# Feed-forward input unscaled, its first 256 columns multiplied tile by tile, the row scale applied behind the product

## Chip, cores and metric

One core of a Trainium2 chip runs the kernel alone. The metric is device time in microseconds (us), the median of the runs shown. Engines: PE (TensorE; PEld its weight loads), DVE (VectorE), ACT (ScalarE), POOL (GpSimd), SP (SyncE, which issues most DMAs).

## What is computed

One decoder layer on 512 prompt rows and 32 sample rows: T = 544 tokens, width 2048, all in 32 bits. A mixer sublayer, then

```
def rmsnorm(x, g):
    y = xf * lax.rsqrt(jnp.mean(xf * xf, axis=-1, keepdims=True) + EPS)
    return y * g
x = x + rmsnorm(out, g_post)                 # end of the mixer
h = rmsnorm(x, g_pre)                        # feed-forward
a = square(relu(einsum('ntd,df->ntf', h, w_up)))      # 2048 -> 8192
y = x + rmsnorm(einsum('ntf,fd->ntd', a, w_down), g_post)
```

## The kernel before

Activations lie transposed: 16 tiles of 128 features by 544 tokens. Every 32-bit product is made of three passes over numbers split into a high and a low part (high x high, high x low, low x high); ACT writes high parts, DVE writes low parts as source minus high. The projections before the feed-forward (up to 578 us) are plain: one unit of weights is 4 tiles by 256 columns.

**Feed-forward.** `w_up` goes in 32 groups of 256 columns, and each group is a Strassen-Winograd product of 2x2 blocks: 7 products (i = 0 to 6, numbered N = 7 G + i), each 8 x 3 matmuls of 272 columns. The block sums of the weights are made by POOL (`t1`, `t3`, `t2`, `t4`, L737 to L756), those of the activations once (`h_sum`, L1504, 8 x 272 = 2176 elements a row), then every part is split (`h_high`, `h_low`, L1509; for weights `high_copy`, `high_part`, `low_part`, L1445). After each product DVE reads the bank (`take`, L1462 and L1465) and adds it to one of four quadrants (`quads`). Products 0, 2, 4 and 6 of a group accumulate in one bank, so product 2 may start only when product 0 has been taken (`taken_before`). At a group's end `square_relu` (L1472, L1474) squares the quadrants, POOL forms their block sums (`activation_sums`, L762 to L767), ACT the high part (`mlp_high`, L1037), DVE the low part (`mlp_low`, L1479), and SP stores both to DRAM (`store_hi`, `store_lo`). `w_down` follows in 64 groups of 7 half-size products.

DVE's order in the up stage is written out by hand; i = 6 is the last product of a group:

```
for N in range(3, N_UP):
    take(N)
    low_part(N + 3)
    if i == 3 and G > 0: mlp_low(G - 1)
    if i == 6: square_relu(G)
```

**Between mixer and feed-forward** (578 to 642 us) the squares of the out-projection are summed by POOL (`add`, L709) and by PE (`turn_sums`), `row_roots` makes the row scale, PE spreads it over the partitions (`spread_scales`), and then tile by tile: POOL or DVE scales the tile, PE transposes the residual input (`second_turn`, 5 transposes, L1595), DVE adds both (L1437), ACT squares, POOL adds the squares. A second row scale comes out of these, `scale_tiles` (L1493) applies it with the gain, and only then the block sums, the splits and the first product begin.

## Time and profile before

| | us |
|---|---|
| median of 3 runs (lowest, highest) | 2060.28 (2059.46, 2060.66) |
| the profiled execution's own time | 2059.49 |
| its span in the trace | 2057.7 |
| PE busy | 1974.6 (96%) |
| DVE, ACT, POOL busy | 1329.2, 1222.3, 926.7 |
| mean granted TensorE clock | 0.971 |

The span is cut by stage with busy times of all engines; a row of the timeline gives start, length, engine, line, and in brackets how long the engine had been idle and what released it. L numbers are lines of the kernel before. A granted clock (PEclk) of 1.00 is 2.4 GHz, 0.50 is 1.2 GHz.

### The profile page before, as it was taken

Reading aid. Unit: us, or ns where it says so; the run is one execution under the profiler, and the core shown is the slowest. Engines: PE = TensorE matmul, PEld = TensorE weight load, DVE = VectorE, ACT = ScalarE, POOL = GpSimd, SP = SyncE. Lnnn points to the kernel's source line nnn. Section 1 sums busy time; section 2 is a strip of 40 time slices with the busy share of each in tenths; the row PEclk is TensorE's granted clock in tenths of the full one; section 3 lists DMA queues with packets and bytes.
Section 4 is the critical chain, followed back from the end, with each engine's and each line's share of the span. In section 5 each row is a group of like instructions: output and inputs, shape, how many; then the busy total and the mean of one; then the engine's idle time right before and its main releaser. Section 6 shows DMA issues by size and latency. Waiting matters only on the chain.

```text
span 2057.7 us, 39370 instructions
## 1 busy us (share of the span) xinstructions
PE 1974.6 (96%) x15412; PEld 1946.8 (95%) x15412; DVE 1329.2 (65%) x1975; ACT 1222.3 (59%) x1787; POOL 926.7 (45%) x635
## 2 busy tenths in 40 slices
PE   7999999999974999999999999989999999999998
PEld 7999999899954899999999999989999999999998
DVE  3455642622247777777777777766666666666687
ACT  5244421422224577777777777767777777777784
POOL 0000022211152576767677676744445544444472
PEclk9999998999965999999999999999999999999999
DMA  5421121242310556565665656795656556565542
GB/s 178 157 68 57 52 78 57 79 173 86 103 65 22 161 187 209 178 200 184 190 199 184 212 178 199 225 328 190 209 181 203 183 180 206 190 212 187 182 159 88
DMA packets 270766, 328.15 MB, mean 159 GB/s; under 512 B 8128, under 2 KB 236872, under 8 KB 268975
## 3 DMA queue, kind: packets, MB, share of 16 engines
q1 hardware_dynamic: 267104, 315.66, 47.1%
q10 hardware_dynamic: 3479, 9.99, 1.4%
q8 instruction: 123, 2.02, 0.4%
q14 instruction: 60, 0.49, 0.1%
HBM read 253.79 MB, written 74.22 MB: 159 GB/s over the span
## 4 chain that ended last, share of the span: by engine, by line
PE 91%; DVE 4%; POOL 2%; issue 1%; DMA 1%; ACT 0%; SPq 0%; DVEq 0%; POOLq 0%; ACTq 0%
PE banks L1629 21%; PE banks L1984 21%; PE banks L1986 21%; PE banks L1985 21%; PE banks L1774 1%; POOL sq_sum L709 1%; PE banks L1595 1%; PE banks L1744 1%; PE banks L1762 1%; DVE h_part L1509 1%; DVE x1T L1493 1%; DVE h_sum L1504 0%; DMA mlp_kept<-mlp_sums 0%; PE banks L2002 0%; PE banks L1816 0%
## 5 line engine op out<-in xcount | busy, mean ns | idle before, releaser
L1984 PE MATMUL banks<-h_part,splits 128*128 128x272 f32 x1792 | 524.4, 293 | 26.9 <-DVE h_part L1509 16.1
L1984 PE MATMUL banks<-mlp_parts,splits 128*128 128x272 f32 x1792 | 518.3, 289 | 5.4 <-DVE y_sum L1462 3.7
L1986 PE MATMUL banks<-h_part,splits 128*128 128x272 f32 x1792 | 522.7, 292 | 0.0
L1985 PE MATMUL banks<-h_part,splits 128*128 128x272 f32 x1792 | 520.2, 290 | 0.0
L1986 PE MATMUL banks<-mlp_parts,splits 128*128 128x272 f32 x1792 | 517.7, 289 | 0.0
L1985 PE MATMUL banks<-mlp_parts,splits 128*128 128x272 f32 x1792 | 516.8, 288 | 0.0
L1984 PEld LDWEIGHTS banks<-h_part,splits 128*128 128x128 f32 x1792 | 341.7, 191 | 28.0 <-issue 19.7
L1984 PEld LDWEIGHTS banks<-mlp_parts,splits 128*128 128x128 f32 x1792 | 337.3, 188 | 6.2 <-issue 3.9
L1985 PEld LDWEIGHTS banks<-h_part,splits 128*128 128x128 f32 x1792 | 342.3, 191 | 0.0
L1985 PEld LDWEIGHTS banks<-mlp_parts,splits 128*128 128x128 f32 x1792 | 341.5, 191 | 0.0
L1986 PEld LDWEIGHTS banks<-h_part,splits 128*128 128x128 f32 x1792 | 341.4, 191 | 0.0
L1986 PEld LDWEIGHTS banks<-mlp_parts,splits 128*128 128x128 f32 x1792 | 337.3, 188 | 0.0
L1465 DVE TENSOR_TENSOR y_sum<-y_sum,banks 128x272 f32<-128x272 f32 x416 | 182.1, 438 | 184.5 <-PE banks L1986 184.4
L1629 PE MATMUL banks<-acts_hi,w_hi 128*128 128x272 f32 x1184 | 253.3, 295 | 9.4 <-DVE uT L1185 4.1
L1629 PE MATMUL banks<-acts_lo,w_hi 128*128 128x272 f32 x1184 | 247.0, 290 | 0.0
L1629 PE MATMUL banks<-acts_hi,w_lo 128*128 128x272 f32 x1184 | 247.0, 290 | 0.0
L803 ACT ACTIVATE w_hi<-w_raw 128x1024 fp32r<-128x1024 f32 x74 | 78.3, 1059 | 283.3 <-PE banks L1629 276.3
L1103 DVE TENSOR_TENSOR w_lo<-w_raw,w_hi 128x1024 fp32r<-128x1024 f32 x74 | 101.5, 1373 | 199.2 <-ACT w_hi L803 198.9
L1629 PEld LDWEIGHTS banks<-acts_hi,w_hi 128*128 128x128 f32 x1184 | 188.0, 191 | 15.5 <-issue 12.3
L1028 ACT ACTIVATE splits<-t_y 128x512 fp32r<-128x512 f32 (+1 forms) x192 | 148.5, 774 | 78.1 <-PE banks L1986 78.1
L1629 PEld LDWEIGHTS banks<-acts_lo,w_hi 128*128 128x128 f32 x1184 | 189.0, 191 | 0.0
L1629 PEld LDWEIGHTS banks<-acts_hi,w_lo 128*128 128x128 f32 x1184 | 187.3, 191 | 0.0
(234 smaller groups left out, 3453.7 us busy)
## 6 DMA issues: line engine op xcount, KB each, us to landing
raw_up<-in_w_up SPq DMA_DIRECT2D x128, 512.0 KB, 7.7
raw_down<-in_w_down SPq DMA_DIRECT2D x128, 512.0 KB, 4.4
mlp_parts<-mlp_kept SPq DMA_DIRECT2D x56, 1088.0 KB, 8.3
mlp_kept<-mlp_hi SPq DMA_DIRECT2D x32, 952.0 KB, 4.5
mlp_kept<-mlp_sums SPq DMA_DIRECT2D x32, 952.0 KB, 5.7
w_raw<-in_w_in SPq DMA_DIRECT2D x40, 512.0 KB, 3.5
w_raw<-in_w_out SPq DMA_DIRECT2D x32, 512.0 KB, 3.3
x_kept<-x1T SPq DMA_DIRECT2D x4, 1088.0 KB, 4.0
```

The lines of the kernel that those rows point to most:

```text
L709: nc.gpsimd.tensor_tensor(total[:], total[:], tmp[:, par * T:(par + 1) * T], ALU.add).then_inc(sq_added, 1)
L803: nc.scalar.activation(w_hi[:, k % SPLIT_SLOTS, :], w_raw[:, k % RAW_SLOTS, :], ACT.Copy).then_inc(hi_split, 1)
L1028: nc.scalar.activation(split_of(N, 0), weight_of(N), ACT.Copy).then_inc(part_hi, 1)
L1103: nc.vector.tensor_tensor(w_lo[:, k % SPLIT_SLOTS, :], w_raw[:, k % RAW_SLOTS, :], w_hi[:, k % SPLIT_SLOTS, :].bitcast(F32), ALU.subtract) ...
L1465: nc.vector.tensor_tensor(dst, dst, src, ALU.add).then_inc(taken, 1)
L1493: ins = nc.vector.scalar_tensor_tensor(out=x1T[:, kt, :], in0=x1T[:, kt, :], scalar=g_ffn[:, kt:kt + 1], in1=norm_scale[:], op0=ALU.mult, ...
L1509: nc.vector.tensor_tensor(h_parts[i][1][:], src, h_parts[i][0][:].bitcast(F32), ALU.subtract).then_inc(hp_lo, 1)
L1595: ins = nc.tensor.transpose(flat(2 * s, T)[:, c * P:c * P + r], tok[0:r, c, kt * P:(kt + 1) * P], ident[0:r, 0:r])
L1629: ins = nc.tensor.matmul(out[:, h, :], w, x[:, h * H:(h + 1) * H], start=first, stop=last)
L1984: nc.tensor.matmul(out, wh, xh, start=first, stop=False, skip_group_check=not STARTS[i])
L1985: nc.tensor.matmul(out, wh, xl, start=False, stop=False, skip_group_check=not STARTS[i])
L1986: ins = nc.tensor.matmul(out, wl, xh, start=False, stop=j == pairs - 1, skip_group_check=not STARTS[i])
```

## The change

The sublayer's input x1 is kept without its row scales: the out-projection gets only its gain; the residual input is multiplied by the row's root mean square instead (`rms`, by ACT, DVE and POOL, `scale_x`), so that x1T holds x1 divided by a row scale s1. Its epsilon is scaled (`eps_1`), s1 comes back at the very end (`s1_col`). Tiles are split high and low as they come (`tile_high`, `tile_low`), and the first 256 columns of `w_up` are multiplied plainly with them, 12 matmuls a tile (`plain_tile`), in place of the first Strassen group; 31 groups are left, on `w_up` columns from 256. The gain is applied to x1T in place (`gain`, POOL and ACT), the four block sums are made behind the plain part by DVE and POOL. The second row scale is summed at N = 4, spread at N = 6, and applied to the products (`ffn_scale`): `square_relu` is now relu times scale over four quadrants, then two squarings. For N < 14 the low part subtracts the high part in SBUF (`split_of`) rather than a copy in PSUM. Weight sum `t3` overwrites a block of the raw weights.

```
-    UP_GROUPS = F // UNIT_N
+    F_GROUPS = F // UNIT_N
+    UP_GROUPS = F_GROUPS - 1
...
+            sp.wait_ge(h_summed[0], 2)
+            sp.wait_ge(h_summed[1], 2)
...
+            blocks_split(0)
+            load_up(2)
+            store_hi(0)
+            store_lo(0)
+            for g in range(1, UP_GROUPS - 1):
+                store_hi(g)
+                store_lo(g)
...
+            def gain(kt):
+                gp.wait_ge(hp_hi, kt + 1)
+                gp.wait_ge(hp_lo, kt + 1)
+                gp.wait_ge(sq_ready, KT + kt + 1)
+                gp.wait_ge(x1_moved[kt // 2], 16)
+                nc.gpsimd.tensor_scalar(x1T[:, kt, :], x1T[:, kt, :], g_ffn[:, kt:kt + 1], None, ALU.mult).then_inc(gained[0], 1)
...
+                gp.wait_ge(t_ready, 4 * G + 1)
+                b12 = block_of(G, 0, 1)
+                nc.gpsimd.tensor_tensor(b12, block_of(G, 1, 1), b12, ALU.subtract).then_inc(t_ready, 1)
...
             t2(0)
+            a11, a12 = x1_quads[:, :, 0, 0, :], x1_quads[:, :, 1, 0, :]
+            a21 = x1_quads[:, :, 0, 1, :]
+            gp.wait_ge(gained[0], KT // 2)
+            gp.wait_ge(gained[1], KT // 2)
+            nc.gpsimd.tensor_tensor(s_sums[4][:], a11, a21, ALU.subtract).then_inc(h_summed[1], 1)
+            gp.wait_ge(unit_used, U_END)
+            gp.wait_ge(h_summed[0], 2)
+            nc.gpsimd.tensor_tensor(s_sums[5][:], a12, s_sums[2][:], ALU.subtract).then_inc(h_summed[1], 1)
             for G in range(ALL_G):
                 t4(G)
                 if 0 < G <= UP_GROUPS:
-                    activation_sums(G - 1)
+                    activation_sums(G)
                 if G + 1 < ALL_G:
                     t1(G + 1)
                     t3(G + 1)
+                    if G == 0:
+                        activation_sums(0)
...
+            def tile_high(kt):
                 act.wait_ge(x1_ready, kt + 1)
...
+                nc.scalar.activation(tile_parts(kt, 0), tile_halves(kt), ACT.Copy, scale=g_ffn[:, kt:kt + 1]).then_inc(hp_hi, 1)
...
+            for N, sums in ((1, (2, 0, 2)), (2, (3, 0, 1)), (3, (4, 1, 2)), (4, (5, 1, 2))):
                 high_copy(N)
                 high_part(N)
...
+                sum_high(*sums)
+            for N in range(5, N_ALL):
                 high_copy(N)
                 high_part(N)
                 G, i = divmod(N, NP)
...
+            step(nc.vector.tensor_copy(s1_col[:], rstd[:]))
+            step(nc.vector.tensor_scalar(eps_1[:], var[:], EPS, None, ALU.mult))
+            nc.vector.tensor_tensor(rms[:], var[:], rstd[:], ALU.mult).then_inc(rms_ready, 1)
...
+            def add_x(kt):
+                dve.wait_ge(x_turned, KT + kt + 1)
+                nc.vector.tensor_tensor(x1T[:, kt, :], x1T[:, kt, :], flat(2 * (kt % 2), T), ALU.add).then_inc(x1_ready, 1)
+            def tile_low(kt):
+                dve.wait_ge(x1_ready, kt + 1)
+                dve.wait_ge(hp_hi, kt + 1)
+                nc.vector.scalar_tensor_tensor(out=tile_parts(kt, 1), in0=tile_halves(kt), scalar=g_ffn[:, kt:kt + 1],
+                                               in1=tile_parts(kt, 0).bitcast(F32), op0=ALU.mult, op1=ALU.subtract).then_inc(hp_lo, 1)
+            def low_part(N):
+                if N >= HIGH_FROM:
+                    dve.wait_ge(hi_copied, N - HIGH_FROM + 1)
                 else:
...
+            def square_quads(g, a21):
+                dve.wait_ge(relued, g + 4)
+                nc.vector.tensor_tensor(mlp_sums[:, 0:3, :], quads[:, 1:4, :] if g > 0 else mlp_sums[:, 0:3, :],
+                                        quads[:, 1:4, :] if g > 0 else mlp_sums[:, 0:3, :], ALU.mult).then_inc(squared, 1)
+                nc.vector.tensor_tensor(a21, a21, a21, ALU.mult).then_inc(squared, 1)
             def square_relu(g):
-                dve.wait_ge(taken, NP * (g + 1))
-                if g > 0:
-                    dve.wait_ge(lo_stored, 16 * g)
-                nc.vector.scalar_tensor_tensor(out=mlp_sums[:, 0:3, :], in0=quads[:, 1:4, :], scalar=0.0, in1=quads[:, 1:4, :],
-                                               op0=ALU.max, op1=ALU.mult).then_inc(squared, 1)
-                nc.vector.scalar_tensor_tensor(out=quads[:, 0, :], in0=quads[:, 0, :], scalar=0.0, in1=quads[:, 0, :],
-                                               op0=ALU.max, op1=ALU.mult).then_inc(squared, 1)
+                dve.wait_ge(taken, NP * g)
+                by_half = quads[:].rearrange("p (a h) n -> p a h n", h=2)
+                nc.vector.scalar_tensor_tensor(out=by_half, in0=by_half, scalar=0.0,
+                                               in1=ffn_scale[:].unsqueeze(1).broadcast_to([P, 2, 2, H]),
+                                               op0=ALU.max, op1=ALU.mult).then_inc(relued, 1)
+                dve.wait_ge(lo_stored, 16 * g)
+                square_quads(g, quads[:, 0, :])
+            def square_relu_plain():
+                dve.wait_ge(h_summed[1], 2)
+                for out, bank, h in ((mlp_sums[:, 0, :], 6, 0), (mlp_sums[:, 1, :], 7, 1), (mlp_sums[:, 2, :], 4, 0),
+                                     (plain21[:], 5, 1)):
+                    nc.vector.scalar_tensor_tensor(out=out, in0=banks[:, bank, 0:H], scalar=0.0, in1=ffn_scale[:, 1 - h, :],
+                                                   op0=ALU.max, op1=ALU.mult).then_inc(relued, 1)
+                square_quads(0, plain21[:])
...
+            def sum_low(i, rounded):
+                dve.wait_ge(hp_hi, rounded)
+                nc.vector.tensor_tensor(s_parts[i][1][:], s_sums[i][:], s_parts[i][0][:].bitcast(F32), ALU.subtract).then_inc(hp_lo, 1)
+            add_x(0)
+            add_x(1)
+            for kt in range(KT):
+                tile_low(kt)
+                if kt + 2 < KT:
+                    add_x(kt + 2)
+                if kt == 5:
+                    split(U_FFN + 2)
+                if kt == 9:
+                    split(U_FFN + 3)
             low_part(0)
+            dve.wait_ge(gained[0], KT // 2)
+            dve.wait_ge(gained[1], KT // 2)
+            nc.vector.tensor_tensor(s_sums[3][:], x1_quads[:, :, 0, 1, :], x1_quads[:, :, 1, 1, :], ALU.add).then_inc(h_summed[0], 1)
+            dve.wait_ge(h_summed[0], 1)
+            nc.vector.tensor_tensor(s_sums[2][:], s_sums[3][:], x1_quads[:, :, 0, 0, :], ALU.subtract).then_inc(h_summed[0], 1)
             low_part(1)
+            dve.wait_ge(h_summed[0], 2)
+            sum_low(2, KT + 1)
             low_part(2)
             take(0)
+            sum_low(3, KT + 2)
+            take(1)
             low_part(3)
+            sum_low(4, KT + 3)
+            take(2)
             low_part(4)
+            sum_low(5, KT + 4)
+            take(3)
             low_part(5)
+            take(4)
+            low_part(6)
+            sums_by_token(2, banks[:, 1, :])
+            row_roots(2, eps_1)
+            take(5)
+            low_part(7)
+            dve.wait_ge(spread, 2)
...
+            dve.wait_ge(scale_ready, 4)
+            square_relu_plain()
+            take(6)
+            low_part(8)
+            low_part(9)
+            mlp_low(0)
+            square_relu(1)
+            for N in range(NP, N_UP):
...
                 G, i = divmod(N, NP)
-                if i == 3 and G > 0:
-                    mlp_low(G - 1)
+                if i == 3:
+                    mlp_low(G)
                 if i == 6:
-                    square_relu(G)
...
+            def plain_tile(kt):
...
+                for nt in range(2):
+                    for w, x, first, last in ((w_hi, 0, kt == 0, False), (w_hi, 1, False, False), (w_lo, 0, False, kt == KT - 1)):
+                        for h in range(2):
+                            ins = nc.tensor.matmul(out[:, h, :], w[s][:, cols], base[:, t + 2 * h, x, j, :], start=first, stop=last)
...
+            for kt in range(KT):
+                if kt + 2 < KT:
+                    second_turn(kt + 2)
+                plain_tile(kt)
...
+                if N == 4:
+                    turn_sums(2, banks[:, 1, :])
+                if N == 6:
+                    pe.wait_ge(rstd_ready, 3)
+                    spread_chunks(lambda c: banks[:, 1, c * P:(c + 1) * P] if c < TOK - 1 else banks[:, 4, 512 - ND:512])
+                if N == NP:
+                    pe.wait_ge(scale_ready, 4)
```

Where order moves. **DVE at the end of an up group, before** (`splits` are the parts of the weights, `quads` the quadrants):

```order
L1462 COPY quads<-banks 128x272 [waits a_summed,product_done]
L1445 TENSOR_TENSOR splits<-t_y,banks 128x1024 [waits product_done,hi_copied]
L1472 SCALAR_TENSOR_TENSOR mlp_sums<-quads 128x816 [waits lo_stored,taken]
L1474 SCALAR_TENSOR_TENSOR quads<-quads 128x272
L1462 COPY quads<-banks 128x272 [waits squared,product_done]
L1445 TENSOR_TENSOR splits<-t_x,banks 128x1024 [waits product_done,hi_copied]
```

The same place now:

```order
L1601 COPY quads<-banks 128x272 [waits a_summed,product_done]
L1582 TENSOR_TENSOR splits<-t_y,banks 128x1024 [waits product_done,hi_copied]
L1616 SCALAR_TENSOR_TENSOR quads<-quads,ffn_scale 128x1088 [waits taken]
L1608 TENSOR_TENSOR mlp_sums<-quads 128x816 [waits relued,lo_stored]
L1610 TENSOR_TENSOR quads<-quads 128x272
L1601 COPY quads<-banks 128x272 [waits squared,product_done]
L1582 TENSOR_TENSOR splits<-t_x,banks 128x1024 [waits product_done,hi_copied]
```

Between the last take of a group and the first take of the next stand three instructions over 2176 columns where two over 1088 stood.

**DVE behind the plain part, now** (`s_sum` block sums, `s_part` their halves):

```order
L1652 TENSOR_TENSOR s_sum_114<-x1T 128x2176 [waits gained_act,gained_pool]
L1654 TENSOR_TENSOR s_sum_113<-s_sum_114,x1T 128x2176 [waits h_summed_dve]
L1582 TENSOR_TENSOR splits<-raw_up_121,splits 128x1024 [waits unit_used,part_hi]
L1637 TENSOR_TENSOR s_part_1_106<-s_sum_113,s_part_0_105 128x2176 [waits hp_hi,h_summed_dve]
L1582 TENSOR_TENSOR splits<-t_y,splits 128x1024 [waits product_done,part_hi]
L1601 COPY quads<-banks 128x272 [waits product_done]
```

and **POOL at the same time**:

```order
L785 TENSOR_SCALAR x1T<-x1T,vecs 128x544 [waits sq_ready,x1_moved7,hp_lo,hp_hi]
L812 TENSOR_TENSOR t_x<-raw_up_121 128x1024 [waits raw_landed0]
L817 TENSOR_TENSOR raw_up_121<-raw_up_121 128x8x128 [waits t_ready]
L824 TENSOR_TENSOR t_y<-raw_up_121,t_x 128x1024 [waits t_ready]
L850 TENSOR_TENSOR s_sum_115<-x1T 128x2176 [waits gained_act,gained_pool]
L853 TENSOR_TENSOR s_sum_116<-x1T,s_sum_113 128x2176 [waits h_summed_dve,unit_used]
L830 TENSOR_TENSOR t_y<-raw_up_121,t_y 128x1024 [waits t_ready,part_lo,part_hi]
```

The low part of the second product's weights now stands behind two block sums on DVE, and two more block sums stand in POOL's queue ahead of `t4`.

## Rows read from the trace of the kernel before

**Rows 1.** The page: the chain that ended last, by engine.
```profile
PE 91%; DVE 4%; POOL 2%; issue 1%; DMA 1%; ACT 0%; SPq 0%; DVEq 0%; POOLq 0%; ACTq 0%
```

**Rows 2.** By stretch: busy PE, PEld, DVE, ACT, POOL; PEclk; DMA share; GB/s.
```profile
585.00:621.00 36.00, 19.23 (x73) 12.98 (x72) 21.98 (x25) 10.38 (x16) 32.19 (x23) 0.50 0.28 114
...
642.00:685.00 43.00, 29.86 (x168) 29.28 (x169) 38.08 (x30) 23.34 (x19) 9.85 (x5) 0.74 0.31 98
685.00:716.00 31.00, 28.74 (x216) 28.55 (x215) 21.98 (x23) 20.28 (x20) 20.46 (x11) 0.94 0.43 132
...
716.00:1330.00 614.00, 613.91 (x4868) 613.72 (x4867) 476.43 (x493) 448.48 (x435) 434.25 (x232) 1.00 0.62 192
```

**Rows 3.** Timeline (start, us, engine, line, tile): ACT, PE, DVE before the feed-forward.
```profile
577.96 0.62 ACT L977 ACTIVATE sq_tmp<-banks 128x544 f32<-128x544 f32 x1 [2.38 <-PE banks L1629]
...
577.76 2.29 PE L1595 MATMUL banks<-ident,x_tok 128*128 128x128 f32 x15
...
582.18 0.16 DVE L1119 COPY ss<-banks 128x4 f32<-128x4 f32 x1 [2.84 <-PE banks L1619]
...
583.89 0.17 DVE L1115 TENSOR_TENSOR rstd<-root,newton 128x5 f32<-128x5 f32 x1
...
587.57 1.35 PE L1595 MATMUL banks<-ident,x_tok 128*128 128x128 f32 x5 [0.82 <-DVE norm_scale L1126]
```

**Rows 4.** PE in the input projection's first pair, tile by tile.
```profile
29.96 1.53 PE L1595 MATMUL banks<-ident,x_tok 128*128 128x128 f32 x10
...
34.54 1.53 PE L1595 MATMUL banks<-ident,x_tok 128*128 128x128 f32 x10
```

**Rows 5.** Groups by shape: busy us, mean ns of one | idle before.
```profile
L1504 DVE TENSOR_TENSOR h_sum<-x1T 128x2176 f32<-128x2176 f32 x2 | 4.8, 2418 | 0.0
...
L737 POOL TENSOR_TENSOR t_x<-raw_up 128x1024 f32<-128x1024 f32 x32 | 77.1, 2410 | 14.6 <-DMA raw_up<-in_w_up 14.6
...
L709 POOL TENSOR_TENSOR sq_sum<-sq_sum,sq_tmp 128x544 f32<-128x544 f32 x30 | 42.4, 1412 | 168.1 <-ACT sq_tmp L977 167.0
...
L693 POOL TENSOR_TENSOR acts_lo<-qT,acts_hi 128x2176 fp32r<-128x2176 f32 x2 | 10.7, 5378 | 29.1 <-ACT acts_hi L947 29.1
...
L699 POOL MEMSET sq_sum<- 128x544 f32 x2 | 1.1, 560 | 5.2 <-PE banks L1619 5.2
```

**Rows 6.** DVE in order of time, end of one up group.
```profile
731.96 1.21 DVE L1445 TENSOR_TENSOR splits<-t_y,banks 128x1024 fp32r<-128x1024 f32 x1
733.09 1.00 DVE L1472 SCALAR_TENSOR_TENSOR mlp_sums<-quads 128x816 f32<-128x816 f32 x1
734.01 2.65 DVE L1474 SCALAR_TENSOR_TENSOR quads<-quads 128x272 f32<-128x272 f32 x1
736.76 0.44 DVE L1462 COPY quads<-banks 128x272 f32<-128x272 f32 x1
```

**Rows 7.** POOL at the same place.
```profile
733.30 3.06 POOL L756 TENSOR_TENSOR t_y<-raw_up,t_y 128x1024 f32<-128x1024 f32 x1 [4.42 <-DVE splits L1445]
```

**Rows 8.** PE at a third product; DVE and PE at an earlier one.
```profile
737.45 0.29 PE L1984 MATMUL banks<-h_part,splits 128*128 128x272 f32 x1
...
692.90 0.44 DVE L1462 COPY quads<-banks 128x272 f32<-128x272 f32 x1
...
693.49 0.36 PE L1984 MATMUL banks<-h_part,splits 128*128 128x272 f32 x1 [2.26 <-DVE quads L1462]
```

**Rows 9.** By stretch, columns as in Rows 2: two stretches for PEclk.
```profile
58.00:62.00 4.00, 2.10 (x17) 1.88 (x16) 3.90 (x6) 1.06 (x1) 0.00 (x0) 1.00 0.72 262
...
696.00:698.00 2.00, 2.00 (x11) 2.00 (x10) 0.00 (x0) 2.00 (x2) 2.00 (x1) 0.50 0.00 0
```

**Rows 10.** ACT, the high part of one group's activations.
```profile
739.89 1.80 ACT L1037 ACTIVATE mlp_hi<-mlp_sums 128x1904 fp32r<-128x1904 f32 x1 [1.17 <-POOL mlp_sums L767]
```

**Rows 11.** DMA issues of the up stage: KB each, median us to landing.
```profile
mlp_kept<-mlp_sums SPq DMA_DIRECT2D x26, 952.0 KB, 5.7
```

**Rows 12.** DVE at the turn from up to down.
```profile
1351.11 1.01 DVE L1472 SCALAR_TENSOR_TENSOR mlp_sums<-quads 128x816 f32<-128x816 f32 x1 [4.22 <-DMA mlp_kept<-mlp_sums]
```

More of the change, by code:

```diff
@@ L124, in hybrid_decoder @@
         rstd = little("rstd", [P, TOK])
+        s1_col = little("s1_col", [P, TOK])
+        rms = little("rms", [P, TOK])
+        eps_1 = little("eps_1", [P, TOK])
         g_pre, g_post = vecs[:, 0:KT], vecs[:, KT:2 * KT]
@@ L338, in hybrid_decoder @@
         mlp_landed = [sem(f"mlp_landed{i}") for i in range(NP)]
-        x1_moved = [sem(f"x1_moved{i}") for i in range(4)]
+        x1_moved = [sem(f"x1_moved{i}") for i in range(8)]
         y_ready = sem("y_ready")
@@ L479, in hybrid_decoder, with x_scaled_by, x_chunk, tile_parts @@
         ALL_G = UP_GROUPS + DOWN_GROUPS
+        X_SCALER = ((0, 0, 1, 1, 2), (0, 0, 2, 2, 2), (0, 0, 2, 2, 2), (0, 0, 2, 2, 2))
+        def x_scaled_by(kg):
+            return [sum(row.count(who) for row in X_SCALER[:kg + 1]) for who in range(3)]
+        def x_chunk(kg, c):
+            return x_tok2[0:tok_rows[c], c, kg * 512:(kg + 1) * 512]
+        def tile_parts(kt, which):
+            return base[:, kt % 2::2, which, kt // 2, :]
+        def tile_halves(kt):
+            return x1T[:, kt, :].rearrange("p (h n) -> p h n", h=2)
         SCORE_AT = (Q_PAIR0 + 1) * K_UNITS
@@ L1012, in source_ready @@
                 if i == 0:
-                    for one, count in landed(G):
-                        act.wait_ge(one, count)
+                    act.wait_ge(*landed(G))
                 if i in T_NEEDS:
@@ L1079, in _ @@
                 act.wait_ge(y_turned, o + 1)
-                nc.scalar.activation(x1_part(o), y_bank(o, o), ACT.Copy).then_inc(x1_copied[0], 1)
+                c = o % TOK
+                nc.scalar.activation(x1_part(o), y_bank(o, o), ACT.Copy, scale=s1_col[0:tok_rows[c], c:c + 1]).then_inc(x1_copied[0], 1)
                 if i == 5:
@@ L1949, in _, with second_turn @@
-            for kt in range(3, KT):
-                second_turn(kt)
-            turn_sums(2, banks[:, 2, :])
-            spread_chunks(2, lambda c: flat(0, T)[:, c * P:c * P + tok_rows[c]])
-            H_READY = (1, 2, 3, 4, 6, 7, 7)
+            pe.wait_ge(tile_read, 2 * P_FFN - 2)
+            turn_sums(1, banks[:, 0, :])
+            def second_turn(kt):
+                for one, count in zip(x_scaled, x_scaled_by(kt // 4)):
+                    pe.wait_ge(one, count)
+                if kt >= 2:
+                    pe.wait_ge(x1_ready, kt - 1)
+                turn_x(x_tok2, kt, kt % 2)
@@ L1994, in _ @@
             pe.wait_ge(taken, N_ALL)
-            for one in x1_moved:
+            for one in x1_moved[0:4]:
                 pe.wait_ge(one, 32)
```

417 lines of the change are left out of this document (222 added, 195 removed).

## Prediction

> **What bounds the kernel now.** The chain of waits comes first: PE holds 91% of it [rows 1], so time is won only where PE stands still or works at half clock, and anything that stops PE costs in full. The busy time by stretch shows where that is [rows 2]. From 716 to 1330 us PE is busy 613.91 of 614.00 us at a granted clock of 1.00: 4868 matmuls, 0.1261 us each, so a group of 168 takes 21.19 us. Only between the out-projection and the third weight group is there slack: 19.23 us busy of 36 at clock 0.50, then 29.86 of 43 at 0.74, then 28.74 of 31 at 0.94. The change works on that stretch, and also on the instructions that close each of the later groups, where nothing stands idle. I price both against one mark: PE's start of the third product of the third 256-column group, before at 737.45 less one group = 716.3 us [rows 8]; in the changed kernel that is the second Strassen group. The profiled execution took 2059.49 us of its own (span 2057.7, 1.8 around it), 0.8 below the median of 2060.28. What a measurement can tell from no change is 0.2%, about 4 us.
>
> **(a) Start of the tiles.** The last square ends at 578.6, PE's sums stand behind 15 transposes that run from 577.76 for 2.29 us, DVE reads them at 582.18, the row scale is done at 584.06, and the first second turn starts at 587.57 [rows 3]. The turns now stand behind the sums. Since the last square would have held the sums until 578.9 anyway (0.3 for the last add of its tile), that gives 1.1 us, but three small operations (`s1_col`, `eps_1`, `rms`, 0.2 each by the 0.17 of the row scale) come behind: `rms` at 583.6. Then scaling a residual chunk 1.5, turn 1.35, add 0.7, high part 0.7, low part 0.8, and 0.75 in all between engines: the first plain tile at 589.4.
>
> **(b) Plain part.** The nearest rows are the input projection, where 10 transposes (two tiles) and 24 matmuls of 272 columns alternate: transposes start at 29.96 and again at 34.54, 4.58 us apart, and take 1.53 of it [rows 4]. Half of it is one tile: 1.52 for 12 matmuls, 0.77 for a turn. Sixteen tiles and 13 further turns: 16 x 1.52 + 13 x 0.77 = 34.3, and 2.5 for the half clock at which it begins: 626.2. POOL has 15 adds of 1.41 here and 12 operations with one input; the latter lie between a memset's 0.56 and the add's 1.41 [rows 5], and I take 0.65, since they read one array like a copy: 29 us, which fits. DVE's two-input operations lie beside them and give up some time, see (c), for which I add 2: plain part ends at **T = 628** (625 to 634).
>
> **(c) From there to the mark.** DVE and POOL exclude each other when both read two SBUF operands: `square_relu`'s second part, 272 columns, takes 2.65 us where its 816 columns take 1.00, because POOL's `t4` runs from 733.30 for 3.06 us, not the mean 2.41 of its like, and the two end within 0.3 us of each other [rows 5 to 7]. So I add these two engines up instead of overlaying them. DVE to the low part of product 6: two block sums and four low parts of them at about 2.3 each (2.418 in [rows 5]) 13.8, six weight low parts at 1.13 now from SBUF, 6.8, five takes at 0.35, 1.7: 22.3. POOL: six weight sums at 2.37 and two block sums between 4.8 (two of the 2.41 for 1024 columns) and 5.378 [rows 5], 10.2: 24.4. From T + 1 that is T + 47.7. The queue matters on both: the two POOL block sums stand ahead of `t4`, and with it of product 3 and behind. Then to the mark (roots by the 582.18 to 584.06 of [rows 3], DVE's by 1.1 us for 1000 columns as in [rows 6], POOL's by 2.41 for 1024 in [rows 5]): roots 1.9, spread 1.6, `ffn_scale` 1.0, plain relu 1.7, squares 1.3, POOL's activation sums 3.1, `t2` 2.4, ACT and DVE split 1.1, `mlp_hi` 1.80 [rows 10], a `t4` in the way 1.9, `mlp_low` 2.0, the store that `square_relu(1)` waits for 5.0 (5.7 median to landing in [rows 11]), squares 1.3, take and PE 0.6: 26.7, and 2.4 for the clock that is cold once after a stall. 47.7 + 26.7 + 2.4 = 76.8, so the mark comes at 704.8, **11.5 us ahead** of 716.3. Ends: 4 ahead (T at 634, the weight sums at 2.6 like their slower ones), 16 ahead (T at 625, two or three microseconds of the two queues side by side).
>
> **(d) Each further group.** Before, the last take of a group is followed by 816 columns (1.00), then 272 that wait for `t4` to 736.66, then the take at 736.76 for 0.44; PE's third product starts at 737.45 [rows 6, 8]. Where PE did wait for that take, it started 0.15 us behind it (693.34 to 693.49) [rows 8]. So the slack before is 737.45 - 737.20 - 0.15 = 0.10 us. Now relu times scale over 1088 columns goes first. It reads quadrants and scale, both in SBUF. The two starts behind each other, 733.09 and 734.01, give 0.92 us for 816 columns, so 272 more cost 0.31. `t4` gets in behind it, 0.31 us later than before, and the squaring of 816 columns (0.92) comes behind `t4`, ahead of the short one and the take. Take(0) of the next group is 0.31 + 0.92 = 1.23 us later, 1.13 beyond the slack. Products 0 and 2 share a bank, so PE stands still for 1.13 us. Nothing makes it good: the next group has the same lengths on all queues, and PE cannot run ahead at 1.00. There are 29 such group ends behind the mark: 29 x 1.13 = **32.8 us lost**. Bounds: 29.0 (1.00 each, `t4` a little shorter) to 36.3 (1.25 each, if `t4` itself stretches with what it meets).
>
> **(e) Turn from up to down.** DVE waits 4.22 us there for a store [rows 12]; loads of the first down weights come later and stores before them. Nothing prices this; PE's buffer of ready parts hides it as before. I take 0, between 4 gained (the wait gone) and 4 lost (one more). Everything else in the change, such as `s1_col` in the last stage, puts one operand in the place of another: nothing.
>
> **Sum.** 2059.5 - 11.5 + 32.8 + 0 = 2080.8, and 0.8 to the median: **2081.6 us**, slower by 1.0%. PE's work itself is nearly equal: 168 matmuls go, 192 come (3 us, inside T).
>
> **Rivals.** *A, the group ends fit (faster).* If relu and both squarings get in before `t4`, or if DVE's 2176 columns lie where PE has more ready than I see, (d) is zero: 2059.5 - 11.5 + 0.8 = 2049. For it: the order of two operations 0.2 us apart decides. Against it: `t4` starts within 0.2 us of the end of the part it waits for [rows 6, 7], and the slack is 0.10 us; it decides once less than 0.15 us a group is lost. Chance 0.12. *B, the front gains three times as much (the same).* If the exclusion in (c) does not hold for ports and the two engines run side by side, DVE's 22.3 us lie beside POOL's 24.4 and the mark comes 22.3 us earlier; with (d) the sum is 2059. Against it: the 2.65 us for 272 columns [rows 6]. Chance 0.08. *C, each stall costs clock too.* After an idle of 2.26 us ahead of 693.49 PE ran at 0.50 from 696 to 698 [rows 8, 9], which costs 1.0 us, and about 0.6 at its edges. Twenty-nine times that would be 46 more: 2128. Against it: from 58 to 62 PE was busy 2.10 of 4.00 us and kept 1.00 [rows 9], and my stall is half as long. Chance 0.04. *D, the plain part stays at half clock.* With only transposes and their gaps PE had 0.50 from 585 to 621 [rows 2]; now turns stand between the plain matmuls. At half clock the matmuls take 24.3 more and 13 turns 7.5 more (1.35 for 0.77), less the 2.5 that I have put in: 2081.6 + 29.3 = 2111. Against it: the mixture of [rows 4] runs 24 matmuls in 3.05 us, full speed. Chance 0.04. The Trainium skill, "TensorE: Matmul & The Clock Gate", section "Part 4: PE-mode transpose", says that a transpose does not count as PE busy the same way, and that the full clock does not engage for it. By that rule alone case D would have more weight; the mixture in the trace speaks against it here. *That the change does not do what it says* (the first group computed twice, say) the order of the instructions excludes: 31 Strassen groups and 192 plain matmuls.
>
> **Numbers.** Forecast 0.72, A 0.12, B 0.08, C 0.04, D 0.04. The forecast's own range is 2072 to 2092 (front 4 to 16, stalls 29 to 36.3, turn 4 each way, not all at one end). To leave out no more than 0.2, the range goes down to A with a little, 2048, and up to 2096. Faster by over 0.2%: A and a part of B, 0.15; within it 0.08; slower 0.77.
>
> **What would show it.** Right: plain part ends near 628; first Strassen product about 14 us later; from the mark on third products 22.3 us apart where they were 21.19; PE idle about 1.1 us once in each group behind a take; PEclk 1.00 from 716 on; the squaring of 816 columns long (about 3.3 us with the wait for `t4`), not the relu and not the 272. Wrong: groups 21.2 us apart (A); a first up product before 630 or a mark before 690 (B); PEclk under 0.9 in the up stage (C); 0.50 from 590 to 640 (D). A down stage that begins with a gap over 4 us would overturn (e).

## The result, and the profile of the changed kernel

| | us |
|---|---|
| changed kernel, median of 4 runs (lowest, highest) | 2095.11 (2093.46, 2096.58) |
| kernel before, beside it, 4 runs | 2059.87 (2058.70, 2060.66) |
| ratio, 95% interval | 1.0171 (1.0159 to 1.0184) |
| span of the profiled execution (before 2057.7) | 2093.3 |
| PE busy, DVE busy (before 1974.6, 1329.2) | 1977.4, 1370.7 |
| mean granted TensorE clock (before 0.971) | 0.976 |

Slower by 35 us, where 21 were forecast. The stated range (2048 to 2096) holds the median with 0.9 us to spare; the range that the forecast's own terms gave (2072 to 2092) does not. PE works as long as before, and at no lower clock. What grew is its waiting. The chain that ended last says where (page, shares of the span), to be read against [rows 1]:

```profile
PE 81%; DVE 12%; issue 3%; POOL 1%; DMA 1%; ACT 1%; SPq 0%; DVEq 0%; POOLq 0%; ACTq 0%
```

PE went from 91% to 81%, DVE from 4% to 12%. The stretches of [rows 2] now (busy PE, PEld, DVE, ACT, POOL; PEclk; DMA share; GB/s):

```profile
585.00:621.00 36.00, 31.47 (x185) 27.51 (x185) 26.88 (x27) 23.09 (x35) 35.43 (x22) 0.79 0.27 104
...
642.00:685.00 43.00, 21.66 (x121) 21.05 (x122) 42.97 (x17) 13.15 (x9) 32.17 (x8) 0.65 0.16 50
685.00:716.00 31.00, 16.44 (x117) 16.08 (x116) 20.29 (x31) 6.85 (x7) 12.58 (x9) 0.79 0.38 131
716.00:1330.00 614.00, 588.60 (x4615) 583.21 (x4615) 481.22 (x493) 424.18 (x411) 422.02 (x221) 1.00 0.56 181
```

Ahead of 642 us PE does more than before (31.47 us in the first stretch where it had 19.23). From 642 to 716 it does less. From 716 to 1330, where it had no gap at all, it is busy 588.60 of 614 us at a clock of 1.00: 25.4 us of standing still, in one place per group. DVE in order of time at that place (start, us, engine, line, tile), answering to [rows 6]:

```profile
909.54 1.21 DVE L1582 TENSOR_TENSOR splits<-t_y,banks 128x1024 fp32r<-128x1024 f32 x1
910.67 1.28 DVE L1616 SCALAR_TENSOR_TENSOR quads<-quads,ffn_scale 128x1088 f32<-128x1088 f32 x1
912.06 3.03 DVE L1608 TENSOR_TENSOR mlp_sums<-quads 128x816 f32<-128x816 f32 x1
915.01 0.43 DVE L1610 TENSOR_TENSOR quads<-quads 128x272 f32<-128x272 f32 x1
915.54 0.44 DVE L1601 COPY quads<-banks 128x272 f32<-128x272 f32 x1
```

POOL there, as in [rows 7]:

```profile
910.88 3.33 POOL L830 TENSOR_TENSOR t_y<-raw_up,t_y 128x1024 f32<-128x1024 f32 x1 [4.41 <-DVE splits L1582]
```

PE at two third products behind each other, as in [rows 8]:

```profile
893.78 0.36 PE L2157 MATMUL banks<-s_part,splits 128*128 128x272 f32 x1 [0.93 <-DVE quads L1601]
...
916.13 0.36 PE L2157 MATMUL banks<-s_part,splits 128*128 128x272 f32 x1 [0.94 <-DVE quads L1601]
```

Relu (1.28 us for 1088 columns) is done at 911.95. `t4` has begun at 910.88 and ends at 914.21. The squaring of 816 columns, which takes 1.0 us alone, lasts 3.03 us and ends at 915.09, 0.9 us behind `t4`. The take starts at 915.54 and PE at 916.13, after 0.94 us of idling. The two third products are 22.35 us apart, where a group took 21.19: 1.16 us each.

Three further places make up the rest. The front, PE (the last row is the mark, the third product of the second Strassen group):

```profile
653.63 0.56 PE L2157 MATMUL banks<-base,splits 128*128 128x272 f32 x1 [15.19 <-ACT splits L1132]
...
712.70 0.57 PE L2157 MATMUL banks<-s_part,splits 128*128 128x272 f32 x1 [14.56 <-DVE quads L1601]
```

The mark stands at 712.70, before at 716.3: 3.6 us gained. How early an execution reaches this stage varies: the last square of the out-projection starts at 577.96 in the trace of the kernel before and at 579.12 here, so of its own the front is 4.8 us shorter. (Over all traces it starts at 576.34 to 580.23.) And the turn from up to down, PE (the first row is the last third product of the up stage):

```profile
1363.13 0.36 PE L2157 MATMUL banks<-s_part,splits 128*128 128x272 f32 x1 [0.94 <-DVE quads L1601]
...
1379.77 0.36 PE L2157 MATMUL banks<-mlp_parts,splits 128*128 128x272 f32 x1 [1.27 <-ACT splits L1132]
...
1388.66 0.57 PE L2157 MATMUL banks<-mlp_parts,splits 128*128 128x272 f32 x1 [5.67 <-DVE y_sum L1601]
```

PE idles 1.27 and 5.67 us ahead of the third product of the down stage, where before it idled 3.66 in all: 3.3 us lost.

**The account** of the two spans: 2093.3 - 2057.7 = 35.6. Front -3.6; from the mark to the last third product of the up stage 1363.13 - 712.70 = 650.43 us, against 29 x 21.19 = 614.5: +35.9, which is 29 x 1.16 = 33.6 and 2.3 once, between the mark and the next third product (737.34, 24.64 us and not 22.35 behind it). Of these 2.3 about 1.7 are clock: PE is at half clock (PEclk 0.50 from 712.70 to 716.50) behind the long wait, 0.23 us a matmul and not 0.126. A single wait of 0.27 us at 727.09 comes to it, and 0.3 is not traced. Turn +3.3. The sum is 35.6.

### The profile page after: what moved, and what is told of

It reads as the page before. It is cut to its first block, busy times and chain, and to the rows that moved or that the text cites. A ratio compares the mean times of both kernels' runs of the same rounds, so it can differ in the third digit from the quotient of the medians.

```text
span 2093.3 us, 39214 instructions
## 1 busy us (share of the span) xinstructions
PE 1977.4 (94%) x15426; PEld 1945.5 (93%) x15426; DVE 1370.7 (65%) x1993; ACT 1214.6 (58%) x1792; POOL 964.7 (46%) x643
## 4 chain that ended last, share of the span: by engine, by line
PE 81%; DVE 12%; issue 3%; POOL 1%; DMA 1%; ACT 1%; SPq 0%; DVEq 0%; POOLq 0%; ACTq 0%
PE banks L1782 21%; PE banks L2157 18%; PE banks L2159 18%; PE banks L2158 18%; DVE mlp_sums L1608 4%; DVE splits L1582 2%; DVE quads L1616 2%; PE banks L1927 1%; PE banks L1748 1%; PE banks L1897 1%; DMA mlp_kept<-mlp_sums 1%; DVE quads L1601 1%; PE banks L1915 1%; POOL sq_sum L767 1%; DVE quads L1610 1%
## 5 line engine op out<-in xcount | busy, mean ns | idle before, releaser
L2157 PE MATMUL banks<-s_part,splits 128*128 128x272 f32 x992 | 292.5, 295 | 51.3 <-DVE quads L1601 49.4
L2159 PE MATMUL banks<-s_part,splits 128*128 128x272 f32 x992 | 289.6, 292 | 0.0
L2158 PE MATMUL banks<-s_part,splits 128*128 128x272 f32 x992 | 287.9, 290 | 0.0
L885 ACT ACTIVATE w_hi<-w_raw 128x1024 fp32r<-128x1024 f32 x78 | 82.5, 1058 | 289.5 <-PE banks L1782 281.8
L2157 PEld LDWEIGHTS banks<-s_part,splits 128*128 128x128 f32 x992 | 189.2, 191 | 57.7 <-issue 56.2
L1225 DVE TENSOR_TENSOR w_lo<-w_raw,w_hi 128x1024 fp32r<-128x1024 f32 x78 | 107.0, 1372 | 203.8 <-ACT w_hi L885 203.5
L2157 PE MATMUL banks<-base,splits 128*128 128x272 f32 x744 | 216.9, 292 | 16.1 <-ACT splits L1132 15.2
L2159 PE MATMUL banks<-base,splits 128*128 128x272 f32 x744 | 216.2, 291 | 0.0
L1132 ACT ACTIVATE splits<-raw_down 128x512 fp32r<-128x512 f32 x256 | 161.7, 632 | 92.9 <-PE banks L2159 92.9
L2158 PE MATMUL banks<-base,splits 128*128 128x272 f32 x744 | 215.1, 289 | 0.0
```

The lines of the kernel that those rows point to most:

```text
L885: nc.scalar.activation(w_hi[k % SPLIT_SLOTS][:], w_raw[:, k % RAW_SLOTS, :], ACT.Copy).then_inc(hi_split, 1)
L1132: nc.scalar.activation(split_of(N, 0), weight_of(N), ACT.Copy).then_inc(part_hi, 1)
L1225: nc.vector.tensor_tensor(w_lo[k % SPLIT_SLOTS][:], w_raw[:, k % RAW_SLOTS, :], w_hi[k % SPLIT_SLOTS][:].bitcast(F32), ALU.subtract).then_ ...
L2157: nc.tensor.matmul(out, wh, xh, start=first, stop=False, skip_group_check=not STARTS[i])
L2158: nc.tensor.matmul(out, wh, xl, start=False, stop=False, skip_group_check=not STARTS[i])
L2159: ins = nc.tensor.matmul(out, wl, xh, start=False, stop=j == pairs - 1, skip_group_check=not STARTS[i])
```

## Experiments

All kernels ran beside the kernel before, on the same chip, its median there 2059.4 to 2059.5. Times are medians; a ratio is against those runs.

**The group ends.** The first question was whether 1.16 us a group comes from the third operation at all, and the second whether from its columns or from `t4`'s place among them. The kernel before with the three operations, in short form:

```
-  stt(mlp_sums[0:3], quads[1:4], 0.0, quads[1:4], max, mult)
-  stt(quads[0], quads[0], 0.0, quads[0], max, mult)
+  stt(quads, quads, 0.0, quads, max, max)
+  tensor_tensor(mlp_sums[0:3], quads[1:4], quads[1:4], mult)
+  tensor_tensor(quads[0], quads[0], quads[0], mult)
```

> The kernel before, with its two squarings of relu replaced by the three operations of the changed kernel (relu over 1088 columns, then squares over 816 and 272), and nothing else. Theory: third products stand 22.3 us apart, PE idle 0.9 us in front of each, 29 to 30 times 1.16 = 34 to 35 us: 2094. So nearly all that the change loses would be reproduced by this part alone. Rival (the loss comes from other parts: weight sum t3 in place, high parts from the other buffer, loads): within 5 us of 2060.

Measured 2093.50 us, ratio 1.0168 (1.0152 to 1.0183). All waits of PE from 700 to 1370 us (sum, times, longest):

```profile
PE banks L1986 <- DVE quads L1463: 28.1, 30, 0.9
```

Thirty waits of 0.94 us: one part of the change, put alone into the old kernel, gives 34 us of its 35. Its groups follow each other at 22.35 us, as in the changed kernel. The other parts therefore nearly cancel (-3.6, +2.3 and +3.3 in the account).

Then the place of `t4`. In the changed kernel:

```
 def t4(G):
+    if 2 <= G <= UP_GROUPS:
+        gp.wait_ge(squared, 2 * G + 2)
```

> The changed kernel, with one wait more on POOL: from the third group on, the weight sum t4 waits until the two squarings of the group's end are done. Theory (each group's end loses 1.16 us because t4 gets in between relu and squarings and holds DVE for 3.0 us): relu 1.28, squaring 0.9 and 0.43 follow each other without a gap, the take comes about 2 us earlier, PE does not wait at the group's end, third products stand 21.19 us apart, t4 takes 2.4 us, and 30 ends give back 30 x 1.16 = 35 less 1.16 for the one at the start: about 2061 us. Rival (the 1088 columns more on DVE are too many wherever t4 stands, or a later t4 makes the next product late): the period stays above 22 us and the time within 5 us of 2095, or the wait moves to the product that reads t4's result.

Measured 2073.91 us, ratio 1.0075 (1.0058 to 1.0092): 21 us back of the 34 expected. DVE at a group's end, and POOL beside it:

```profile
902.86 1.29 DVE L1618 SCALAR_TENSOR_TENSOR quads<-quads,ffn_scale 128x1088 f32<-128x1088 f32 x1
904.25 1.01 DVE L1610 TENSOR_TENSOR mlp_sums<-quads 128x816 f32<-128x816 f32 x1
...
905.71 0.44 DVE L1603 COPY quads<-banks 128x272 f32<-128x272 f32 x1
```

```profile
905.69 2.40 POOL L832 TENSOR_TENSOR t_y<-raw_up,t_y 128x1024 f32<-128x1024 f32 x1 [5.84 <-DVE quads L1612]
```

The squaring takes 1.01 us, `t4` 2.40, and the take comes at 905.71, 2.9 us behind relu's start where it was 4.9. So the collision is gone, and no wait of PE stands at the third product any more. But groups are 21.52 us apart, not 21.19. The rest sits elsewhere, ACT:

```profile
911.19 1.80 ACT L1146 ACTIVATE mlp_hi<-mlp_sums 128x1904 fp32r<-128x1904 f32 x1 [2.71 <-POOL mlp_sums L843]
```

The last activation sum ends at 911.16 because all four stand behind `t4`; `mlp_hi` waits 2.71 us for it, and every later high part stands behind `mlp_hi` in ACT's order. DVE then makes `mlp_low` later, and a take behind that stops PE for 0.26 us. The wait had been moved, partly as the rival said. Next, the order was turned round instead (POOL's loop over the groups):

```
-    t4(G)
+    if G < 2: t4(G)
     if 0 < G <= UP_GROUPS: activation_sums(G)
+    if G >= 2: t4(G)
```

> The changed kernel; from the third group on POOL makes the activation sums first and the weight sum t4 behind them. Theory (with t4 merely held back the period fell to 21.52 us and not 21.19, because the activation sums came 1.5 us later behind t4, and with them mlp_hi on ACT, whose next high parts stand behind it): with the sums first they are done at the place where they were, mlp_hi no later, third products 21.19 us apart, 9 us less than the run with t4 held back: 2065. Rival (the remaining 0.33 us comes from t4 being late itself or from the 1088 columns more on DVE): the period stays at 21.5, 2074.

Measured 2063.60 us (10 runs), ratio 1.0019 (1.0010 to 1.0029). POOL:

```profile
903.21 0.78 POOL L836 TENSOR_TENSOR mlp_sums<-quads,mlp_sums 128x272 f32<-128x272 f32 x1 [6.60 <-DVE quads L1613]
...
906.29 2.43 POOL L830 TENSOR_TENSOR t_y<-raw_up,t_y 128x1024 f32<-128x1024 f32 x1
```

From 716 to 1340 us the list of PE's waits is empty, and DVE's squarings are 21.19 us apart (901.77, 922.96). The 1088 columns more on DVE are all still there, so they cost nothing as such. What cost 31.5 us between the medians (33.5 between the two traces, where 29 groups at 1.16 make 33.6) was that a POOL operation got in among them. At 2063.60 the change is still 0.2% slower than the kernel before. The kernel before with the same order tells whether that order is worth something by itself:

> The kernel before, with POOL's activation sums ahead of t4 from the third group on, the edit that gave the changed kernel 31 us. Theory (in the kernel before DVE's group end just fits, with 0.10 us of slack, so there is nothing to give back): 2060, within 3 us. Rival (the order on POOL is worth something by itself, and the version with all edits owes its lead over before to it): 2055 or less.

Measured 2058.43 us (10 runs), ratio 0.9997 (0.9988 to 1.0006): nothing to give back there.

**The plain part.** POOL in the changed kernel, two of its rows:

```profile
584.76 10.98 POOL L777 TENSOR_SCALAR x_tok<-x_tok,rms 32x512 f32<-32x512 f32 x7 [2.12 <-DVE rms L1553]
...
637.91 3.25 POOL L785 TENSOR_SCALAR x1T<-x1T,vecs 128x544 f32<-128x544 f32 x2
```

Ten residual chunks took 16.1 us (1.6 each) and eight gains 16.5 us (2.1 each). The price of a chunk is not DVE's doing: the first four took 6.4 us, and DVE stood still for 2.2 of them (585.90 to 588.08). DVE's first block sum waits for the last of them, 6.12 us. First the gains were given to ACT (8 of POOL's `gain` calls moved to ACT's list, the waits on `gained` with them):

> The changed kernel, with the eight in-place gain multiplications of POOL (2.1 us each in the trace) given to ACT, which does all sixteen. Theory (POOL's one-input operations, 1.6 to 2.1 us each and not 0.65, pace the plain part and end 6.7 us behind it): POOL's last add at about 624, plain part ends at 628 instead of 634.5, block sums start at about 631 instead of 641.2, the mark (third product of the second Strassen group, 712.7) 8 to 10 us earlier: 2086. Rival (DVE or ACT pace the tiles, and what ends the stage is the same): plain part ends at 634 and the mark moves less than 3 us.

Measured 2088.67 us, ratio 1.0144 (1.0129 to 1.0159): 6.4 us less. DVE's first block sum and PE at the mark:

```profile
635.68 3.41 DVE L1646 TENSOR_TENSOR s_sum<-x1T 128x2176 f32<-128x2176 f32 x1 [1.14 <-ACT x1T L1100]
...
707.36 0.56 PE L2151 MATMUL banks<-s_part,splits 128*128 128x272 f32 x1 [14.57 <-DVE quads L1596]
```

This execution reached the stage 1.2 us later (first turn at 587.86, not 586.64), so the block sum came 6.7 us earlier and the mark 6.6. The plain part itself did not come to 628: from its first matmul to the first Strassen product it took 42.4 us, for 44.1. What it waited for is in ACT's waits of the changed kernel, 585 to 635:

```profile
ACT sq_tmp L1059 <- POOL sq_sum L767: 7.3, 7, 2.8
```

ACT's squares wait for POOL's adds. So six of the ten chunks went too (an entry 2 is a chunk of POOL, 0 one of ACT):

```
-  X_SCALER = ((0, 0, 1, 1, 2), (0, 0, 2, 2, 2), (0, 0, 2, 2, 2), (0, 0, 2, 2, 2))
+  X_SCALER = ((0, 0, 1, 1, 2), (0, 0, 2, 2, 2), (0, 0, 0, 0, 0), (0, 0, 0, 0, 0))
```

> The changed kernel with all gains on ACT, as before, and besides with the six residual chunks of the third and fourth quarter scaled by ACT (0.64 each) and not by POOL (1.6 to 1.9 each). Theory (POOL's one-input operations pace the plain part: ACT's squares wait up to 3.0 us for POOL's adds): those waits go, the plain part takes 38 us from its first matmul and not 42.4 (with gains on ACT) or 44.1 (changed kernel), the mark 4 us earlier than with gains on ACT alone: 2085. Rival (ACT is full now, or DVE's two-input operations against the adds pace it): no more than 1 us.

Measured 2085.49 us, ratio 1.0127 (1.0112 to 1.0142). ACT's waits from 585 to 632, and PE at the first plain matmul, the first Strassen product and the mark:

```profile
ACT base L1090 <- DVE x1T L1558: 5.0, 7, 1.6
ACT x_tok L1085 <- DVE rms L1548: 1.5, 1, 1.5
ACT w_hi L880 <- PE banks L2102: 0.5, 1, 0.5
```

```profile
590.97 1.24 PE L2102 MATMUL banks<-base,w_hi 128*128 128x272 f32 x4 [0.42 <-DVE base L1563]
...
631.09 0.36 PE L2151 MATMUL banks<-base,splits 128*128 128x272 f32 x1 [0.21 <-issue]
...
702.50 0.57 PE L2151 MATMUL banks<-s_part,splits 128*128 128x272 f32 x1 [14.57 <-DVE quads L1596]
```

The waits for POOL are gone, the plain part takes 40.1 us (38 expected), and the mark comes 10.2 us earlier than in the changed kernel, which reached the stage at the same 586.64. DVE's first block sum starts at 632.11 and not 641.20.

**Do DVE and POOL exclude each other?** Behind the plain part DVE's rows were these:

```profile
641.20 4.56 DVE L1652 TENSOR_TENSOR s_sum<-x1T 128x2176 f32<-128x2176 f32 x1 [6.12 <-POOL x1T L785]
645.79 4.44 DVE L1654 TENSOR_TENSOR s_sum<-s_sum,x1T 128x2176 f32<-128x2176 f32 x1
650.16 3.37 DVE L1582 TENSOR_TENSOR splits<-raw_up,splits 128x1024 fp32r<-128x1024 f32 x1
653.45 7.08 DVE L1637 TENSOR_TENSOR s_part<-s_sum,s_part 128x2176 fp32r<-128x2176 f32 x1
660.46 5.81 DVE L1582 TENSOR_TENSOR splits<-t_y,splits 128x1024 fp32r<-128x1024 f32 x1
```

POOL's two block sums lay beside them, from 652.41 for 5.84 us and from 658.21 for 6.98. The experiment made those two on DVE (the edit in words):

```
+  (DVE, behind sum_low(3)) s_sums[4] = x1_quads a11 - a21
+  (DVE, ahead of sum_low(4)) s_sums[5] = x1_quads a12 - s_sums[2]
-  (POOL) the same two
```

> The changed kernel, with the two block sums of POOL (2176 columns, 5.84 and 6.98 us) made by DVE instead, ahead of the takes that follow. Theory (DVE and POOL exclude each other, so their times add up; the same sum costs 5.1 us on POOL and 2.3 on DVE): DVE has 4.8 us more of its own, POOL 10.2 less, the mark comes 3 to 5 us earlier, 2091. Rival (the two work side by side and each is only slowed somewhat): DVE is the longer queue and 4.8 us more on it put the mark 3 to 5 us later, 2099.

Measured 2093.17 us, ratio 1.0166 (1.0151 to 1.0181). DVE:

```profile
642.16 4.56 DVE L1648 TENSOR_TENSOR s_sum<-x1T 128x2176 f32<-128x2176 f32 x1 [6.12 <-POOL x1T L785]
...
654.41 2.41 DVE L1633 TENSOR_TENSOR s_part<-s_sum,s_part 128x2176 fp32r<-128x2176 f32 x1
656.75 1.21 DVE L1578 TENSOR_TENSOR splits<-t_y,splits 128x1024 fp32r<-128x1024 f32 x1
...
660.57 4.62 DVE L1657 TENSOR_TENSOR s_sum<-x1T 128x2176 f32<-128x2176 f32 x1
```

The low part of a block sum takes 2.41 us where it took 7.08, and the low part of the second product's weights 1.21 where it took 5.81. Only beside `t1`, `t3`, `t2` and `t4` are DVE's rows still long (4.56, 4.62). From the first block sum the mark is 69.2 us away (642.16 to 711.33), where it was 71.5: 2.3 us gained, less than the 3 to 5 expected. That it is a gain at all speaks for adding the two queues up: if they ran side by side, the longer queue on DVE was to put the mark 3 to 5 us later. What took the place of the gain is a new wait on POOL: the load of the next raw weights stands behind the last block sum in SP's queue, and POOL's `t1` waits for it, to 677.70, where it started at 673.65 in the changed kernel:

```profile
677.70 3.35 POOL L812 TENSOR_TENSOR t_x<-raw_up 128x1024 f32<-128x1024 f32 x1 [14.79 <-DMA raw_up<-in_w_up]
```

**The turn.** SP in the changed kernel there (start, us, queue, line, tile, count):

```profile
1369.69 1.27 SPq L582 DMA_DIRECT2D raw_down<-in_w_down  x2
...
1375.78 1.74 SPq L597 DMA_DIRECT2D mlp_kept<-mlp_sums  x1
```

The store of `mlp_sums` leaves behind a load, 2.2 us after `mlp_low` was done. I held that for the cause:

> The changed kernel; at the turn from up to down SP issues the store of the last but one low part ahead of the second load of down weights, not behind it. Theory (at the turn the store left SP at 1375.8 though mlp_low was done at 1373.6, and DVE and PE wait for its landing): the store is issued 2.2 us earlier, PE's wait in front of the third product of the down stage falls from 5.67 to about 3.7, 2 us in all: 2093. Rival (the load that is now later stops PE instead, or the store lands no sooner beside the part loads): within 0.5 us of 2095.

Measured 2095.34 us, ratio 1.0176 (1.0161 to 1.0192): nothing. The store left SP at 1373.14, 2.2 us earlier relative to the last third product (1362.68), DVE no longer waited for it, and PE's wait did not move:

```profile
1388.28 0.57 PE L2157 MATMUL banks<-mlp_parts,splits 128*128 128x272 f32 x1 [5.68 <-DVE y_sum L1601]
```

DVE's wait for the store had been 0.26 us only in the changed kernel; another stood beside it. ACT, changed kernel:

```profile
1378.34 0.60 ACT L1123 ACTIVATE banks<-raw_down 128x512 fp32r<-128x512 f32 x1 [7.11 <-DMA raw_down<-in_w_down]
```

The weights of the down stage are requested at 1369.7, and in the kernel before at 1320.93. With 31 Strassen groups in place of 32, the last group lies in the other of the two raw buffers, the one that the first down weights overlay, so they can be loaded only when it has been split. To test that without the rest, the kernel before was given its loads late:

```
                 elif g == UP_GROUPS - 2:
                     blocks_split(g)
-                    load_down(0)
-                    load_down(1)
...
+                if i == 3:
+                    sp.wait_ge(product_done, N_UP - NP + 2)
+                    load_down(0)
                 if i == 4:
+                    load_down(1)
```

> The kernel before, with the first two loads of down weights issued where the changed kernel issues them (behind the third part load of the last up group, some 10 us behind the second product of the last group, instead of 10 us ahead of it). Theory (31 groups end in the other of the two raw buffers, so these loads come about a group later, ACT waits 7.1 us for the weights and DVE's queue behind it, and that is the 3.3 us lost at the turn): PE waits 5.5 us in front of the third product of the down stage and 1.3 us ahead of it, where before it waited 3.66, about 3 us in all: 2062.5. Rival (the loss at the turn hangs on the squarings or on the store): less than 1 us.

Measured 2064.67 us, ratio 1.0030 (1.0017 to 1.0042). PE at its turn:

```profile
1346.00 0.37 PE L1986 MATMUL banks<-mlp_parts,splits 128*128 128x272 f32 x1 [2.47 <-ACT splits L1030]
...
1355.12 0.57 PE L1986 MATMUL banks<-mlp_parts,splits 128*128 128x272 f32 x1 [4.36 <-DVE y_sum L1464]
```

PE waits 2.47 and 4.36 us, 6.83 in all against 3.66 before: 3.2 us, the amount of the changed kernel. The split between the two waits is not the one I had expected, the sum is. The median is 5.2 us longer, more than these waits. The traced execution is the fastest of six (2062.0, the slowest 2068.55), so what the slower ones lose besides is not shown.

**All edits together.**

> All edits together on the changed kernel: gains and half of the chunks on ACT, four block sums on DVE, activation sums ahead of t4, store ahead of load at the turn. If the terms add (6.4 measured for the gains, 1.9 for the block sums, and as forecast 4 for the chunks, 30 for the order on POOL, 2 for the turn): 2095 - 44 = 2051, 0.4% faster than the kernel before. If the terms overlap at the turn or the front is held by another wait: 2055 to 2062.

Measured 2048.64 us, ratio 0.9950 (0.9933 to 0.9966): faster than both kernels by more than the runs scatter. The single terms, 31.5 for the order on POOL, 9.6 for gains and chunks, 1.9 for the block sums and nothing for the store, would have given 2052. The mark in its trace:

```profile
698.40 0.56 PE L2153 MATMUL banks<-s_part,splits 128*128 128x272 f32 x1 [12.79 <-DVE quads L1595]
```

That is 17.9 us ahead of the kernel before's 716.3 (0.7 of it by reaching the stage earlier). So the change can be turned into a gain, but only with both edits, POOL relieved at the front and its order changed in the groups: the order alone gave 2063.60, the gains and chunks alone 2085.49. What this version still loses is the turn (5.52 us of waiting ahead of the third product there) and the 12.79 us of waiting at the mark, of which DVE's wait for the first store is 3.30; neither was tried further.

## Why the prediction came out as it did

- **(d), each further group: right, by mechanism and by size.** 1.13 us times 29 was forecast, 1.16 was measured, behind a squaring of 3.03 us (3.3 forecast), with `t4` stretched to 3.33, the clock at 1.00 and PE idle 0.94 us behind the take (1.1 forecast). The third operation alone gives it, and taking `t4` out from among the three takes it back. One sentence of the working, "Nothing makes it good", spoke of the kernel as it stands. A changed order on POOL does make it good.
- **(c), the two queues: right as a sum.** From the start of the block sums to the mark 75.8 us were forecast (T + 1 to T + 76.8), 71.5 measured: 44.5 and not 46.7 to the low part of product 6 (done at 685.67), then 27.0 and not 29.1. The exclusion on which it rests shows in 7.08 against 2.41 us for the same operation. The single terms of the list behind product 6 were not each measured.
- **(b), the plain part: the step that failed.** It was "12 operations with one input ... and I take 0.65, since they read one array like a copy". There are 18 of them, ten chunks and eight gains, and they took 1.6 and 2.1 us. That is above the upper end that I had drawn, POOL's two-input add of 1.41, so the bound did not hold either. POOL therefore had 33 us of them and not 7.8, was busy from 584.8 to 641.2 without a gap, held ACT's squares up to 2.8 us, and let the block sums begin at 641.2 where T + 1 = 629 had been forecast. With the eight gains and six chunks on ACT they began at 632.11, 9.1 us of these 12.2:

```profile
632.11 3.43 DVE L1646 TENSOR_TENSOR s_sum<-x1T 128x2176 f32<-128x2176 f32 x1 [1.12 <-ACT x1T L1100]
```

- **(a), the start of the tiles: right but for two small terms.** The first plain matmul came at 591.0, not 589.4. The stage was reached 1.2 us later than in the trace of the kernel before; from the last square to `rms` 4.8 us were needed, for 5.0 forecast; and from `rms` to the matmul 6.5, for 5.8. In DVE's queue the second tile's add, which waits for a second turn at half clock, stands ahead of the first tile's low part, and PE waited for that (0.49 us):

```profile
589.30 0.72 DVE L1563 TENSOR_TENSOR x1T<-x1T,banks 128x544 f32<-128x544 f32 x1 [0.50 <-PE banks L1748]
589.94 0.95 DVE L1568 SCALAR_TENSOR_TENSOR base<-x1T,vecs,base 128x544 fp32r<-128x544 f32 x1
```

- **The front as a whole.** These 1.6 us are part of the 12.2. With the 4.3 us that (c) came out shorter, the front gained 3.6 and not 11.5.
- **Clock: one term short.** Behind the 14.56 us wait at the mark PE worked at half clock once more, which is most of the 2.3 us lost there once. The forecast had one such loss ahead of the mark and none behind it. The full clock in the mixture of turns and matmuls held, once PE had worked at half clock to about 597 (PEclk 0.50 from 591 to 594, 0.57 from there to 597.5):

```profile
600.00:630.00 30.00, 26.22 (x180) 23.37 (x179) 24.07 (x25) 20.01 (x31) 29.43 (x18) 0.94 0.35 129
```

The Trainium skill ("TensorE: Matmul & The Clock Gate", "Part 4: PE-mode transpose") says that the full clock does not engage for transposes and that they do not count as PE busy in the same way; read as holding for the mixture too, it would have left the plain part at half clock. The trace speaks against that reading here: PEclk was 0.94, and from 597 on five transposes took 0.77 us between the plain tiles, not the 1.29 that they had taken at 594.
- **(e), the turn: inside its bound, with the sign open.** 3.3 us lost, for "I take 0, between 4 gained (the wait gone) and 4 lost (one more)". Of the two things named, "loads of the first down weights come later" was the cause. That "PE's buffer of ready parts hides it as before" did not hold, and by the prediction's own sign, "a gap over 4 us" at the start of the down stage, this term is overturned: PE stood still for 5.67 us.
- The sum of the misses is 7.9 (front) + 2.3 (clock) + 0.8 (29 x 0.03) + 3.3 (turn) = 14.3 us, the whole distance between 21.3 and 35.6. All four have the same sign, which "not all at one end" had ruled out for the forecast's own range (2072 to 2092). That the stated range still holds the result is luck: its upper end was moved from 2092 to 2096 to leave out less chance, by no term of the sum.
- **Signs.** The period (22.35), the long squaring, the idle PE behind each take and PEclk 1.00 came as written. "Plain part ends near 628" and "first Strassen product about 14 us later" did not: it ended at 634.6, and the first Strassen product followed 0.6 us behind it (635.18): its operand is `base`, the tiles themselves, and no block sum.
- **Rivals.** A (no stall) and B (engines side by side) fell with the rows above, and C (clock lost at every stall) with PEclk 1.00 from 716 on. Where A's condition was brought about, by POOL's order alone, the time was 2063.60 and not A's 2049, since the other terms had been missed too (13.5 of the 14.3 us above). That the version with all edits measures 2048.64 is a coincidence: its front gains far more than A had, and its turn loses.

## What to carry over

When an engine's last steps before a wait of PE are split into more instructions, ask which operation of another engine can start between them and lengthen them, here POOL's `t4`: more columns cost nothing here, an operation that slipped in between them cost 31 us. Before a held-back operation is called free, follow what stands behind it in its own queue: `t4` held back brought 21 us, `t4` behind its neighbours 31.5. A changed number of loop rounds also changes which of two buffers is the last, and with that when the next stage's loads can start.
